# Conformer/pooling trunk on 8 cores: a causal depthwise convolution in two time phases, regrouped in SBUF before the output product

## The reference

```python
def conformer_conv(x, w_in, b_in, w_dw, b_dw, ln_g, ln_b, w_out, b_out):
    h = jnp.einsum('bsd,de->bse', x, w_in) + b_in          # (B, S, 2D)
    val, gate = jnp.split(h, 2, axis=-1)
    h = val * jax.nn.sigmoid(gate)
    h = lax.conv_general_dilated(h, w_dw, window_strides=(1,), padding=[(30, 0)],
        dimension_numbers=('NWC', 'WIO', 'NWC'), feature_group_count=D_MODEL) + b_dw
    h = jax.nn.silu(layer_norm(h, ln_g, ln_b))
    return jnp.einsum('bsd,de->bse', h, w_out) + b_out
def swiglu(x, w_gate, w_up, w_down):                      # D_FF = 2816
    h = jax.nn.silu(jnp.einsum('bsd,df->bsf', x, w_gate)) * jnp.einsum('bsd,df->bsf', x, w_up)
    return jnp.einsum('bsf,fd->bsd', h, w_down)
for i in range(4):
    mix = conformer_conv(x, ...) if i % 2 == 0 else multiscale_pool(x, ...)
    x = layer_norm(alpha * x + mix, ln1_g[i], ln1_b[i])
    x = layer_norm(alpha * x + swiglu(x, ...), ln2_g[i], ln2_b[i])
```

## Time and profile before

| | |
|---|---|
| three timed runs | 2463.82, 2464.4 (median), 2469.79 us |
| the profiled execution | 2459.99 us, span of its slowest core (core 6) 2458.4 us |
| spans of the 8 cores | 2448.9 to 2458.4 us, granted clock 0.993 to 0.994 |
| PE, DVE, ACT, POOL busy | 97%, 62%, 45%, 9% of the span |

### The profile page before, as it was taken

One profiled execution on the slowest core, in us unless ns is written; L12 is line 12 of the kernel. 1 busy time (PEld: TensorE's weight loads), 2 busy tenths in 40 slices (PEclk: granted clock), 3 DMA queues, 4 the chain that ended last, 5 costly groups with the idle time before them and its releaser, 6 DMA issues.

```text
span 2458.4 us, 32245 instructions; the slowest of 8 cores (2448.9 to 2458.4 us)
## 1 busy us (share of the span) xinstructions
PE 2388.4 (97%) x12412; PEld 1074.1 (44%) x12412; DVE 1532.9 (62%) x2372; ACT 1114.9 (45%) x1656; POOL 216.9 (9%) x410
## 2 busy tenths in 40 slices
PE   5989999999999999999999999999999999999996
PEld 2333444444444444444444444444444444444444
DVE  3457577378837883735774726764885588555255
ACT  4557554434353534464453654551626253624033
POOL 1000111010000000000000000001000001010110
PEclk9999999999999999999999999999999999999998
DMA  9996985444535454467753476654444435466653
GB/s 198 181 169 112 177 149 93 69 81 70 89 67 84 67 85 68 83 118 134 134 86 66 77 144 120 120 92 74 75 76 75 76 66 89 71 107 139 99 96 99
DMA packets 112456, 250.35 MB, mean 102 GB/s; under 512 B 12080, under 2 KB 55088, under 8 KB 112304
## 3 DMA queue, kind: packets, MB, share of 16 engines
q0 software_dynamic: 58464, 191.92, 46.8%
q1 hardware_dynamic: 53840, 56.38, 10.5%
HBM read 419.17 MB, written 16.78 MB: 177 GB/s over the span
## 4 chain that ended last, share of the span: by engine, by line
PE 93%; DMA 3%; issue 2%; DVE 2%; ACT 0%; SPq 0%; POOL 0%; DVEq 0%; POOLq 0%; ACTq 0%
PE ps L875 93%; DMA ud<-sb_ust 1%; DMA sb_R<-x 1%; DMA sb_x<-ud 1%; DMA sb_wM<-wout 1%; DVE sb_R L454 0%; DVE sb_R L452 0%; SPq L652 0%; ACT sb_xT L783 0%; ACT sb_R L478 0%; DVE sb_hT L426 0%; DVE sb_lnQ L426 0%; DVE sb_R L474 0%; POOL sb_wM L346 0%; DVE sb_hT L424 0%
## 5 line engine op out<-in xcount | busy, mean ns | idle before, releaser
L875 PE MATMUL ps<-sb_xT,sb_wF 128*128 128x512 bf16 x5632 | 1233.8, 379 | 5.6 <-ACT sb_xT L467 3.7
L875 PEld LDWEIGHTS ps<-sb_xT,sb_wF 128*128 128x128 bf16 x5632 | 549.8, 98 | 683.6 <-issue 23.4
L875 PE MATMUL ps<-sb_hT,sb_wF 128*128 128x512 bf16 x2640 | 582.6, 379 | 0.0
L553 DVE TENSOR_TENSOR sb_hT<-ps,sb_sgF 128x512 bf16<-128x512 f32 x352 | 243.2, 691 | 451.1 <-PE ps L875 442.3
L551 ACT ACTIVATE sb_sgF<-ps 128x512 f32<-128x512 f32 x352 | 210.0, 597 | 534.0 <-PE ps L875 526.6
L875 PEld LDWEIGHTS ps<-sb_hT,sb_wF 128*128 128x128 bf16 x2640 | 256.6, 98 | 317.8 <-issue 12.5
L417 ACT ACTIVATE sb_lnX<-sb_R 128x512 f32<-128x512 f32 (+1 forms) x231 | 140.6, 615 | 373.5 <-DVE sb_R L532 204.2
L532 DVE TENSOR_TENSOR sb_R<-sb_R,ps 128x512 f32<-128x512 f32 (+1 forms) x264 | 177.1, 671 | 165.3 <-PE ps L875 163.9
L875 PE MATMUL ps<-sb_xT,sb_wM 128*128 128x512 bf16 x1024 | 234.8, 388 | 31.7 <-ACT sb_xT L783 23.3
L346 POOL DMA_DIRECT2D sb_wF<-wgu x198 | 104.7, 529 | 1108.5 <-PE ps L875 1104.3
L478 ACT ACTIVATE sb_R<-sb_R,sb_cst 128x512 f32<-128x512 f32 (+1 forms) x256 | 192.5, 796 | 7.6 <-DVE sb_R L454 7.1
(11 more groups left out here) (85 smaller groups left out, 1293.3 us busy)
## 6 DMA issues: line engine op xcount, KB each, us to landing
sb_wF<-wgu POOLq DMA_DIRECT2D x198, 512.0 KB, 5.5
sb_wF<-wd POOLq DMA_DIRECT2D x120, 352.0 KB, 4.7
sb_x<-ud SPq DMA_DIRECT2D x192, 135.0 KB, 6.4
sb_wM<-win POOLq DMA_DIRECT2D x32, 512.0 KB, 7.5
sb_wM<-wout POOLq DMA_DIRECT2D x32, 512.0 KB, 6.5
ud<-sb_ust SPq DMA_DIRECT2D x64, 128.0 KB, 6.0
y<-sb_R SPq DMA_DIRECT2D x12, 512.0 KB, 9.2
sb_R<-x SPq DMA_DIRECT2D x8, 512.0 KB, 17.5
```

Of the source, the lines that this page charges most:

```text
L553: S.op("dve", lambda e: e.tensor_tensor(out=hT[:, jj, h * NT:(h + 1) * NT], in0=ps[:, bu, :], in1=sgF[:, i, :], op=ALU.mult), reads=[("PS" ...
L875: r = self.e.matmul(*a, **k)
```

## The change

The convolution works on even and odd steps apart. `conv_in` writes a tile as two phases of 256 steps, with 15 steps of history in front (copied from the previous tile, or from `uh` between pairs) and zeros behind: 288 values, 576 bytes a row (`XW`). `ud` has a row of 8 channels in a piece (4608 bytes) for each phase, and `conv_taps` loads, per phase, 4 shifts x 16 rows of 2300 values (4600 bytes): two loads a block in place of four. Partitions now hold 2 phases x 4 shifts x 16 rows. A block's 32 products give 16 channels x 2 output phases in 32 columns over 256 steps: 2 halves `h` x 4 steps `m` x 4 groups `g`, written in that order. The tap table `lag` is its own bf16 tensor, loaded once for each conv layer by POOL. In `Y` a partition now holds one output phase of two channels, so ACT evicts and applies Silu in halves with their own bias columns, `phase_finish` sums over partitions of the same phase (`samem`) and works on 256 columns, and two transfers a chunk (line 763 of the changed kernel) regroup the bf16 result so that a partition holds one channel's two phases; `conv_out` multiplies that, with the rows of `w_out` put in the matching order, and the add to `R` reads PSUM phase by phase. The norms lower the boost by `STEP` a tile, so that subtraction, product and output of a tile come one after the other in the order; the last half-quarter norms take two chunks in one DVE operation, and of their scalings only two go to DVE. `commit` no longer waits for a buffer's last writer where it waits for that writer's readers. In the planner DVE operations are shorter (0.63) and the landings of stores to `ud` and tap loads longer (`lat` 2.5 and 4.0).

```diff
@@ -24,7 +24,7 @@
 ...
-XW = NT + 28
+XW = NH + 32
 ...
@@ -143,9 +143,10 @@
 ...
         for w in writes:
-            if w in self.last_w:
+            if self.readers.get(w):
+                deps.extend(self.readers[w])
+            elif w in self.last_w:
                 deps.append(self.last_w[w])
-            deps.extend(self.readers.get(w, ()))
 ...
@@ -233,12 +234,13 @@
 ...
-    ud = {L: dram(f"ud{L}", [8, 128, SEQ], kind="Internal", dt=BF16) for L in (0, 2)}
+    ud = {L: dram(f"ud{L}", [2, 8, 4, 16, 8 * XW], kind="Internal", dt=BF16) for L in (0, 2)}
 ...
@@ -251,9 +253,10 @@
 ...
-        x4 = sb("x4", [128, NX4, 4, XW], BF16)
+        x4 = sb("x4", [128, NX4, 8 * XW], BF16)
 ...
-        ust = sb("ust", [128, 3, NT], BF16)
+        ust = sb("ust", [128, 3, 2, XW], BF16)
+        uh = sb("uh", [128, 8, 2, 16], BF16)
 ...
@@ -286,7 +290,7 @@
 ...
-        DV = 0.72
+        DV = 0.63
 ...
@@ -294,8 +298,12 @@
 ...
+        def load_lags(l, after):
+            S.op("pool", lambda e: e.dma_start(out=lag[:], in_=lag_d[l]), reads=after, writes=[("LAG",)],
+                 dma=f"d_lag{l}", dur=0.6, size=262144)
@@ -404,7 +412,7 @@
 ...
-            return DV if n == NT else 0.42
+            return DV if n == NT else 0.36
 ...
@@ -426,6 +434,46 @@
 ...
+        def phase_finish(st, tiles, banks, out):
+            bm, bq = banks
+            s_, q_, sk, qk = sums(st)
+            for t, k in ((s_, sk), (q_, qk)):
+                S.op("dve", lambda e, t=t: e.tensor_tensor(out=t[:, 0:NH], in0=t[:, 0:NH], in1=t[:, NH:NT],
+                                                           op=ALU.add), reads=k, writes=k, dur=tt(NH))
+            s_, q_ = s_[:, 0:NH], q_[:, 0:NH]
 ...
+                return e.matmul(ps[:, bq, 0:NH], samem, q_, start=True, stop=True)
+            S.op("pe", mm, reads=sk + qk + [("C0",)], writes=[("PS", bm), ("PS", bq)], dur=0.9)
 ...
+            S.op("dve", lambda e: e.tensor_tensor(out=q_, in0=ps[:, bq, 0:NH], in1=lnX[:, i, 0:NH],
+                                                  op=ALU.subtract),
 ...
+            sw = s_.unsqueeze(1).to_broadcast([128, 2, NH])
+            qw = q_.unsqueeze(1).to_broadcast([128, 2, NH])
+            S.boost += 8 * STEP
+            for c in range(8):
+                z, zk = tiles[c]
+                zw = z.rearrange("p (b n) -> p b n", b=2)
+                S.op("dve", lambda e, zw=zw: e.tensor_tensor(out=zw, in0=zw, in1=sw, op=ALU.subtract),
+                     reads=list(zk) + sk, writes=zk, dur=DV)
+                S.op("dve", lambda e, zw=zw: e.tensor_tensor(out=zw, in0=zw, in1=qw, op=ALU.mult),
+                     reads=list(zk) + qk, writes=zk, dur=DV)
+                out(c)
+                S.boost -= STEP
+        STEP = 0.7
 ...
@@ -447,6 +495,22 @@
 ...
                  reads=qk, writes=qk, dur=0.7, table="exp", boost=2 * EVICT)
+            if n == NH:
+                S.boost += 8 * STEP
+                for c in range(0, 8, 2):
+                    (z, zk), (_, zk1) = tiles[c], tiles[c + 1]
+                    at = z.offset % z.ap[0][0] - c * SEQ
+                    zw = R[:, c:c + 2, at:at + NH]
+                    ks = list(zk) + list(zk1)
+                    for w, wk, op in ((s_, sk, ALU.subtract), (q_, qk, ALU.mult)):
+                        S.op("dve", lambda e, zw=zw, w=w, op=op: e.tensor_tensor(
+                            out=zw, in0=zw, in1=w.unsqueeze(1).to_broadcast([128, 2, NH]), op=op),
+                            reads=ks + wk, writes=ks, dur=DV)
+                    out(c)
+                    out(c + 1)
+                    S.boost -= 2 * STEP
+                return
+            S.boost += 8 * STEP
 ...
@@ -470,7 +535,7 @@
 ...
-            if part is not None and c % 2:
+            if part == 1 and c in (3, 7):
 ...
@@ -619,11 +685,26 @@
 ...
             i = flip("ust", 3)
-            S.op("dve", lambda e: e.scalar_tensor_tensor(out=ust[:, i, :], in0=tgt[:], scalar=1.0, in1=vbt[:],
-                                                         op0=ALU.add, op1=ALU.mult),
-                 reads=[("TG",), ("VB",)], writes=[("US", i)], dur=DV)
-            S.op("sp", lambda e: e.dma_start(out=ud[L][c, :, q * NT:(q + 1) * NT], in_=ust[:, i, :]),
-                 reads=[("US", i)], writes=[("UD", L, c, q)], dma=f"d_us{i}", dur=0.45, size=131072, lat=1.0)
+            head = ust[:, i, :, 0:15]
+            if q == 0:
+                S.op("dve", lambda e: e.memset(head, 0.0), writes=[("UX", i)], dur=0.1)
+            elif q == 2:
+                S.op("dve", lambda e: e.tensor_copy(out=head, in_=uh[:, c, :, 0:15]),
+                     reads=[("UH", c)], writes=[("UX", i)], dur=0.1)
+            else:
+                j = (i + 2) % 3
+                S.op("dve", lambda e: e.tensor_copy(out=head, in_=ust[:, j, :, NH:NH + 15]),
+                     reads=[("US", j)], writes=[("UX", i)], dur=0.1)
+            S.op("dve", lambda e: e.scalar_tensor_tensor(
+                out=ust[:, i, :, 15:15 + NH], in0=tgt[:].rearrange("p (n f) -> p f n", f=2), scalar=1.0,
+                in1=vbt[:].rearrange("p (n f) -> p f n", f=2), op0=ALU.add, op1=ALU.mult),
+                reads=[("TG",), ("VB",)], writes=[("US", i)], dur=DV)
+            S.op("sp", lambda e: e.dma_start(
+                out=ud[L][:, c, q].rearrange("f k (g w) -> (k g) f w", g=8), in_=ust[:, i]),
+                reads=[("US", i), ("UX", i)], writes=[("UD", L, c, q)], dma=f"d_us{i}", dur=0.45, size=139264, lat=2.5)
+            if q == 1:
+                S.op("dve", lambda e: e.tensor_copy(out=uh[:, c, :, 0:15], in_=ust[:, i, :, NH:NH + 15]),
+                     reads=[("US", i)], writes=[("UH", c)], dur=0.1)
 ...
@@ -639,42 +720,50 @@
 ...
-            if q == 0:
-                S.op("dve", lambda e: e.memset(x4[:, i, :, 0:32], 0.0), writes=[("X4", i, s) for s in range(4)],
-                     dur=0.15)
-            for s in range(4):
-                o = q * NT - 28 - s
-                z = max(0, -o)
-                src = ud[L][c, :, o + z:o + XW].rearrange("(g p) w -> p g w", g=4)
-                S.op("sp", lambda e, s=s, z=z, src=src: e.dma_start(out=x4[s * 32:(s + 1) * 32, i, :, z:XW],
-                                                                    in_=src),
-                     reads=[("UD", L, c, q)] + ([("UD", L, c, q - 1)] if q else []), writes=[("X4", i, s)],
-                     dma=f"d_x4_{i}_{s}", dur=0.55, size=138240, lat=3.0)
 ...
+            for f in range(2):
+                row = ud[L][f, c, q]
+                src = bass.AP(row.tensor, row.offset, [[1, 4], [8 * XW, 16], [1, 8 * XW - 4]])
+                S.op("sp", lambda e, f=f, src=src: e.dma_start(out=x4[f * 64:(f + 1) * 64, i, 0:8 * XW - 4], in_=src),
+                     reads=[("UD", L, c, q)], writes=[("X4", i, f)], dma=f"d_x4_{i}_{f}", dur=0.55, size=277000, lat=4.0)
 ...
                 ins = None
-                for m in range(8):
-                    for g in range(4):
-                        ins = e.matmul(ps[g * 32:(g + 1) * 32, b, :], wt[:, m * 4 + g, :],
-                                       x4[:, i, g, 28 - 4 * m:28 - 4 * m + NT], start=(m == 0), stop=(m == 7))
+                for h in range(2):
+                    for m in range(4):
+                        for g in range(4):
+                            ins = e.matmul(ps[g * 32:(g + 1) * 32, b, h * NH:(h + 1) * NH], wt[:, m * 8 + 2 * g + h, :],
+                                           x4[:, i, (2 * g + h) * XW + 12 - 4 * m:(2 * g + h) * XW + 12 - 4 * m + NH],
+                                           start=(m == 0), stop=(m == 3))
                 return ins
-            S.op("pe", mm, reads=[("X4", i, s) for s in range(4)] + wk, writes=[("PS", b)], dur=1.9)
-            S.op("act", lambda e: e.activation(out=y, in_=ps[:, b, :], func=AF.Identity,
-                                               bias=col(f"bdw{l}", c), scale=1.0),
-                 reads=[("PS", b), ("C0",)], writes=yk, dur=0.74)
+            S.op("pe", mm, reads=[("X4", i, s) for s in range(2)] + wk, writes=[("PS", b)], dur=1.1)
+            for h in range(2):
+                S.op("act", lambda e, h=h: e.activation(out=y[:, h * NH:(h + 1) * NH], in_=ps[:, b, h * NH:(h + 1) * NH],
+                                                        func=AF.Identity, bias=col(f"bdw{l}", 2 * c + h), scale=1.0),
+                     reads=[("PS", b), ("C0",)], writes=yk[h:h + 1], dur=0.48)
 ...
             def out(c):
-                S.op("act", lambda e: e.activation(out=yt[1][c], in_=yt[0][c], func=AF.Silu,
-                                                   bias=col(f"lnb{l}", c), scale=col(f"lng{l}", c)),
-                     reads=yt[2][c] + [("C0",)], writes=yt[2][c], dur=0.86, table="silu")
-            ln_finish(bk["st"], [(yt[0][c], yt[2][c]) for c in range(8)], bk["ln"], out)
+                y, yb, (tk, dk) = yt[0][c], yt[1][c], yt[2][c]
+                for h in range(2):
```

(20 more changed lines are left out.)

91 lines of the change are left out of this document (63 added, 28 removed).

## The result

The changed kernel takes 2566.0 us (median of 4 runs, 2557.2 to 2570.3), the kernel before 2464.1 beside it (4 runs). The ratio is 1.040, with a 95% interval of 1.037 to 1.044. The forecast was 2448 with a range of 2410 to 2525: the time lies outside it, on the side of the rival "four engines at the loaded rate".

A forecast was written before the change was run, and what follows sets the result against it. TensorE's products were taken as the bound, busy 2388.4 of 2458.4 us. From 2460.0: −39 products, −4 end, +28 late tap loads, 0 first 300 us gave 2445, put at 2448 as a median; range 2410 to 2525.

The forecast's parts named there:

- four engines at the loaded rate: Rival, chance 0.30: tap loads on four engines slowed by weight traffic, late in blocks 4 to 8; about 2520 to 2571 us.
- which engines: Tap loads: with four shifts outermost a load may use 4 of 16 DMA engines, 147.2 KB each; with 16, 36.8 KB.
- what the changes on PE and at the end are worth: Shorter tap and conv norm products after 300 us, −39 us; wide last norms at the end, −4 (bounds −1 and −7).
- all landings in time: Rival, chance 0.22: tap loads use all engines or the order has room; 2407 to 2417, median about 2415 us.
- the stall term: Late tap loads on four engines: 9.3 us per pair of spans, three pairs behind the front, +28 us.
- Tap loads: Least sure term: two loads of 589 KB a block in place of four of 135 KB; +28, or +129 at E 10.8.
- late by 5E − 26.7: Second span of taps, layer 2: load 8 lands after it is wanted by this much, 6.3 us at E of 6.6.
- E: An engine's time for one block's tap loads with four engines: between 6.1 and 10.8 us, taken as 6.6.
- late by 3E − 16.8: First span of taps: load 7 lands after it is wanted by this much, 3.0 us at E of 6.6.
- All of it is PE time: Tap load lateness, 9.3 us a pair, counts wholly as PE time, since PE takes its products in order.
- The front: First 300 us: shorter products against landings, regrouping and longer tap loads; taken as 0, bounds −22 and +25 us.
- It decides from E = 7.2: Threshold in the four-engine rival: lateness outweighs the 43 us gain only from E 7.2 us, below 20.4 GB/s per engine.

The follow-up runs named there:

- experiments 1 and 2: 1 is k16, 2413.8 us on its second chip; 2 is k2, k4_x4, k8 and k16_x4: 2889.3, 2555.9, 2437.6 and 2445.3 us.
- the series of 2, 4, 8 and 16: Changed kernel with four tap loads a block, outermost count 2, 4, 8 or 16: 2889.3, 2555.9, 2437.6, 2445.3 us.
- k8: Changed kernel with four tap loads a block, each 8 rows outermost, then 4 shifts: 2437.6 us, beside 2462.1 for the kernel before.
- k16_x4: Changed kernel with four tap loads a block, each 16 rows outermost, then 2 shifts: 2445.3 us, ratio 0.990 to the kernel before.
- k16: Changed kernel with tap loads' 16 rows outermost in place of 4 shifts: 2410.3 us, on another chip 2413.8, ratio 0.979 to the kernel before.
- experiment 6: Stores to `ud` issued by ACT instead of SP: on the changed kernel 2570.8 us, ratio 1.041; on k16 2437.2, ratio 0.986.
- experiment 4: Kernel before with its 32 tap products of 512 columns made 256 wide, half the taps left out: 2439.1 us, ratio 0.991.
- 5: k16 with two parts undone separately: the planner's earlier numbers, 2416.7 us, ratio 0.980; without the 128 regrouping transfers, 2410.3 us, ratio 0.978.
- k2: Changed kernel with four tap loads a block, each 2 shifts outermost, then 16 rows: 2889.3 us, beside 2462.1 for the kernel before.
- k4_x4: Changed kernel with four tap loads a block, each 4 shifts outermost, then 8 rows: 2555.9 us, ratio 1.038 to the kernel before.

## Why the prediction was wrong, step by step

**Right: which engines.** "The source names four shifts outermost ... With 4 it is 147.2 KB per engine": shown by experiments 1 and 2. By the Trainium skill ("DMA: Bandwidth & Descriptors", Why a DMA increments its semaphore by 16 and not by 1) the outermost counts decide; the series of 2, 4, 8 and 16 agrees, in packets up to 16 and in time up to 8 (PE waits 18 to 23 us for tap loads in k8, by core, and 9.0 in k16_x4).

**Right: what the changes on PE and at the end are worth.** The start of the 5600th gate or up product, counted in the trace, is 2409.2 before, 2370.7 in k16 and 2524.2 in the changed kernel. k16 gains 38.5 there and 4.7 in the end behind it; the sum had 39 after 300 us, 0 in front, 4 at the end. The rival "all landings in time" put it at 2415, and k16 takes 2413.8. PE is busy 2335.1 us in it, 9 over the 2326 forecast. A block takes 0.99 us from its start to the next product (1206.11 to 1207.10), at 1.06 forecast. The two kinds of halves on ACT are 0.469 and 0.593, at 0.48 and 0.591.

**Wrong: the stall term, +28 forecast.** Its parts, each as the changed kernel against k16 (the same order), by the start of the same product; in brackets the taps that lie between:

| at the start of | changed | k16 | lost since the row above |
|---|---|---|---|
| gate/up product 1 (first pair of layer 0) | 242.1 | 202.6 | 39.5 |
| product 800 (its second pair) | 628.3 | 544.3 | 44.5 |
| 2000 (no taps) | 1027.0 | 943.1 | −0.1 |
| 2800 (layer 2, first pair) | 1418.6 | 1300.7 | 34.0 |
| 3600 (second pair) | 1850.4 | 1698.0 | 34.5 |
| 5600 (no taps) | 2524.2 | 2370.7 | 1.1 |

A pair was to cost 9.3 and cost 34.0 to 44.5. The three pairs that the term covers cost 113 us in place of 28, and the fourth, in the front, 39.5 where it had none. Four things were mis-sized, the first three in "Tap loads":

- *The second span*, "late by 5E − 26.7": the form held. E was 7.4, not 6.6. Load 4 may start at 1299.3, when block 1 has ended, and block 4 runs at 1313.1: 13.8 after it, so 6.4 beside E and not the latency of 3 that I took from small stores at the quiet end. With both, 1.1 + 37.0 + 6.4 − 30.8 = 13.7; measured are 44.5 us from block 1 to block 8 against 31.0 in k16, 13.5. That 6.4 are the latency of a four-engine load is read from this one place; the trace has no landing of such loads.
- *The first span*, "late by 3E − 16.8", 3.0: it was 20.3. The sum looked at the loads alone. That a load needs its store, and that the store needs the same four engines, was left out; the store's landing went from 6.1 to 11.5, and DVE, whose three `ust` buffers come free with it, waited 109 us. In the span itself 10.5 are waits for tap loads, 6.1 waits behind stores, and 3.7 slower products (experiment 6). How much of the 10.5 is a load that was itself issued late, behind a store, was not separated.
- *"All of it is PE time"*: it is, but a wait costs more than its length. Waits are 103 us of the loss and slower products 50, by the two pages, so a microsecond of added wait went with 1.5 of loss. Nothing in the sum stood for the clock, though the front of the kernel before had it in a row (0.97 in its first 300 us).
- *The front*, "Bounds −22 and +25; I take 0": product 1 starts at 242.1 where it started at 201.1 before, +41.0 and beyond the upper bound; in k16, at 202.6, the 0 holds. The same loads are late here (before product 1 PE waits 26.0 us for them in place of 0.7, and 12.3 once for the regrouping `sb_hT`, which lands in 10.2 us in place of 4.4), and the bound of one landing more for each of two spans was too small.

**The rival that came out** had the right place and the wrong size for it: it needed E of 9 to 10.8 for 2520 to 2571, and 2566 came with E of 7.4. "It decides from E = 7.2" was the costly sentence. With the measured 7.4 the sum's own form gives 10.3 + 5.4 = 15.7 a pair and 47 for three, a time of about 2464: the error in E is 19 us, and the rest of the miss is what the form left out. Four engines at 7.4 cost 152 us in four pairs, against the 49 that k16 gains. By that form an E of 6.6 would take 8 × 0.8 = 6.4 us a pair off, 26 in all (an estimate), and not change the side: with four engines the forecast's branch was not open, and its chance belonged to the slower side.

**The smaller ones.** Weight loads hide (experiment 4). The regrouping costs nothing that can be told from the spread (5). "None before the first three" blocks of a span held in the spans after 300 us. The first wait for a tap load in a span came at the fifth or sixth block already, and not at the last only. The landing of 9 to 14 us could not be read, as the profile has none for these loads; with 16 engines it is 6.6, where 5 was forecast.

## What to carry to other kernels

Before counting bytes of a transfer, read the outermost count of its address pattern on both sides: with 2 or 4 here, most of the 16 engines' time was unused while TensorE waited, and putting the rows outermost gave 152 us back at the same order and the same bytes. When a stall is priced, ask what else must pass the same engines (the stores that feed these loads), and price the microseconds behind it at the clock that the rows show after a wait. A product made shorter is worth its full size only if the order leaves room for what it waits for: in the dense order the shorter blocks brought 24 us of the 35 or more that were counted, in the spread one the whole sum of 39 came.

## What the runs showed of the hardware beyond what was expected

Stores that are spread over all engines land later beside narrow loads, also from a queue of their own: issued by another engine, in 11.6 us beside four-engine loads and in 6.3 beside sixteen-engine ones. Behind loads of the same queue their median is 15.1, 8.7, 6.4 and 5.9 us with 2, 4, 8 and 16 engines (k2, k4_x4, k8, k16_x4). The weights on Pool's queue do not show it over the whole span: a load of `sb_wF` from `wgu` lands in 5.5 us in the changed kernel and 5.2 in k16.

One engine moved 19.9 GB/s of 4600-byte rows when four were used and 23.2 when two were. These are averages with the pauses in them: the packet itself lasts 178 ns in both stretches (median), and 268 in k16 from 1195 to 1215. And after a wait of 8.4 us, at a granted clock of 0.62, the same 32 products took 1.90 us in place of 1.06.
